# An eleventh weight load split into quarters, two loads held behind the x2 stores, and a top-8 instruction for the choice of experts (one Trainium2 core)

## The reference

```python
def _hmoe(x, g, w_router_group, w_router_expert, w_gate, w_up, w_down):
    xn = _rmsnorm(x, g).reshape(b * l, dm)
    lg = xn @ w_router_group                     # 4 groups
    grp = argmax(lg); wg = max(softmax(lg))
    le_sel = (xn @ w_router_expert)[token, grp]  # 8 experts of the group
    top_v, top_i = lax.top_k(le_sel, 2)
    wk = softmax(top_v) * wg[:, None]
    for e in range(32):
        h = silu(xn @ w_gate[e]) * (xn @ w_up[e])
        y = y + combine[:, e:e + 1] * (h @ w_down[e])
    return x + y
```

## Time and profile before

| what | value |
|---|---|
| median of 3 runs (lowest, highest) | 868.24 us (867.67, 870.07) |
| the profiled execution's own time | 868.5 us |
| span of the profiled execution | 866.9 us |
| TensorE matmul busy | 778.7 us (90%) |
| VectorE, ScalarE, GpSimd busy | 310.0, 136.1, 129.4 us |
| moved by DMA in all | 253.81 MB |
| mean granted TensorE clock | 0.965 |

### The profile page before, as it was taken

One profiled execution on the slowest core, in us unless ns is written; L12 is line 12 of the kernel. 1 busy time (PEld: TensorE's weight loads), 2 busy tenths in 40 slices (PEclk: granted clock), 3 DMA queues, 4 the chain that ended last, 5 costly groups with the idle time before them and its releaser, 6 DMA issues.

```text
span 866.9 us, 9613 instructions
## 1 busy us (share of the span) xinstructions
PE 778.7 (90%) x3736; PEld 430.0 (50%) x3737; DVE 310.0 (36%) x818; ACT 136.1 (16%) x274; POOL 129.4 (15%) x220
## 2 busy tenths in 40 slices
PE   4999999999999999989999878887977977989876
PEld 4888888778877455533333333323323323333222
DVE  4799879624465544631111101101111110111115
ACT  5110021321222333300000000000000000000013
POOL 3000027650233100001111101001000000010100
PEclk9999999999999999999999999889888999989999
DMA  8348033162500790779999999999999999999955
GB/s 283 86 159 139 0 112 100 54 233 92 194 1 1 321 411 27 276 292 422 425 426 425 429 426 426 428 425 427 428 425 428 425 426 429 426 416 407 414 202 246
DMA packets 50784, 253.81 MB, mean 293 GB/s; under 512 B 17829, under 2 KB 18681, under 8 KB 38674
## 3 DMA queue, kind: packets, MB, share of 16 engines
q1 hardware_dynamic: 43778, 239.80, 69.3%
q0 software_dynamic: 6672, 12.86, 4.1%
q10 hardware_dynamic: 288, 0.53, 0.2%
HBM read 246.44 MB, written 14.58 MB: 301 GB/s over the span
## 4 chain that ended last, share of the span: by engine, by line
PE 61%; DMA 31%; SPq 5%; DVE 1%; issue 1%; ACT 1%; POOL 0%; DVEq 0%; ACTq 0%; POOLq 0%
DMA arena<-in_w_exp_up 25%; PE ps L1874 13%; PE ps L1587 13%; PE ps L1650 12%; PE ps L1747 6%; PE ps L1891 6%; SPq L512 3%; PE ps L1963 3%; DMA arena<-x_rows 3%; DMA x_rows<-arena 1%; SPq L516 1%; DMA arena<-in_x_prompt 1%; PE ps L1687 1%; PE ps L1680 1%; PE ps L1864 1%
## 5 line engine op out<-in xcount | busy, mean ns | idle before, releaser
L1874 PE MATMUL ps<-arena 128*64 128x512 f32 x1024 | 249.5, 642 | 55.4 <-DMA arena<-in_w_exp_up 55.3
L1874 PEld LDWEIGHTS ps<-arena 128*64 128x64 f32 x1024 | 81.8, 147 | 200.7 <-issue 192.7
L1891 PE MATMUL ps<-arena 128*64 128x512 f32 x512 | 116.4, 595 | 2.0 <-DVE arena L1485 2.0
L1587 PE MATMUL ps<-arena 128*128 128x272 f32 x480 | 110.8, 393 | 0.0
L1650 PE MATMUL ps<-arena 128*128 128x272 f32 x448 | 105.7, 394 | 1.8 <-ACT arena L758 0.9
L1587 PEld LDWEIGHTS ps<-arena 128*128 128x128 f32 x480 | 91.0, 190 | 18.6
L1489 DVE TENSOR_SCALAR arena<-ps,arena 128x512 f32<-128x512 f32 x32 | 24.0, 751 | 201.1 <-PE ps L1891 201.1
L1650 PEld LDWEIGHTS ps<-arena 128*128 128x128 f32 x448 | 83.9, 190 | 22.3 <-DVE arena L1260 2.6
L1454 DVE TENSOR_TENSOR arena<-ps,arena 128x1024 f32<-128x1024 f32 x15 | 18.4, 1225 | 173.3 <-PE ps L1864 173.3
L907 DVE TENSOR_TENSOR arena<-arena 128x256 f32<-128x256 f32 (+11 forms) x217 | 74.6, 344 | 13.5 <-ACT arena L816 3.9
L857 ACT ACTIVATE arena<-ps,arena 128x512 f32<-128x512 f32 x32 | 22.0, 687 | 306.1 <-PE ps L1874 306.1
(11 more groups left out here) (234 smaller groups left out, 552.7 us busy)
## 6 DMA issues: line engine op xcount, KB each, us to landing
arena<-in_w_exp_gate SPq DMA_DIRECT2D x28, 2048.0 KB, 42.3
arena<-in_w_exp_up SPq DMA_DIRECT2D x28, 2048.0 KB, 32.3
arena<-in_w_exp_down SPq DMA_DIRECT2D x27, 2048.0 KB, 37.9
arena<-in_w_in SPq DMA_DIRECT2D x6, 2048.0 KB, 8.8
arena<-in_w_exp_gate SPq DMA_DIRECT2D x16, 512.0 KB, 11.0
arena<-in_w_exp_up SPq DMA_DIRECT2D x16, 512.0 KB, 18.5
arena<-in_w_exp_down SPq DMA_DIRECT2D x6, 1024.0 KB, 18.4
arena<-in_x_prompt SPq DMA_DIRECT2D x8, 512.0 KB, 9.3
```

Of the source, the lines that this page charges most:

```text
L1587: last = pe.matmul(dst[:, hh, 0:HALF], w[:, k, m * P:(m + 1) * P], rhs[:, k, hh * HALF:(hh + 1) * HALF], start=(k == 0), stop=(k == kk - 1))
L1874: last = pe.matmul(ps[n * TILE:(n + 1) * TILE, 2 + par, :], x_t[:, k, :], w[:, k, :], start=(k == 0), stop=(k == KD - 1))
L1891: last = pe.matmul(ps[half * TILE:(half + 1) * TILE, 6 + par, :], h[par][:, k, :], w_down[:, k, half * F:(half + 1) * F], start=(k == 0), ...
```

## The change

Four edits. (1) Load 10 is cut in four quarters, each of which covers one x2 tile of x_tok. Quarter q is issued when the store of tile q has landed, and the tile has been transposed and squared; three of them stand on SP ahead of load 7, the fourth behind load 9. (2) Loads 8 and 9 also wait until all five x2 stores have landed. (3) POOL waits for the store before, ahead of each x2 store. (4) `choose` takes the two best with `dve.max` (eight largest of a row, sorted) and `dve.max_index` (their positions); `inverse_root` in `norm` becomes a cheaper average of the root and mean/root, whose factor of 2 is put in where rstd is used; one of `keep_busy`'s four rounds goes.

```diff
 def in_quarters(l):
-    return l >= NS and held_before(l) // 3 < QUARTERED and held_before(l) % 3 != 2
+    return l == NS - 1 or l >= NS and held_before(l) // 3 < QUARTERED and held_before(l) % 3 != 2
...
+            def load_over(n):
+                sp.wait_ge(x2_stored, 16 * (n + 1))
+                sp.wait_ge(x2_turned, 2 * n + 2)
+                sp.wait_ge(squares2, 2 * n + 2)
+                q = OUT_ORDER[n]
+                load(NS - 1, slice(q * QUARTER, (q + 1) * QUARTER))
+
+            for n in range(1, TT - 1):
+                load_over(n)
             sp.wait_ge(out_done, 2 * TT - 1)
             load(EARLY)
             sp.wait_ge(out_done, 2 * TT)
+            sp.wait_ge(x2_stored, 16 * TT)
             for l in range(EARLY + 1, NS - 1):
                 load(l)
-            sp.wait_ge(xg_in[0], 16)
-            load(NS - 1)
+            load_over(TT - 1)
...
+                if n:
+                    pool.wait_ge(x2_stored, 16 * n)
                 pool.dma_start(x2_rows[i * P:i * P + ROWS[i]], x_tok[:ROWS[i], i, :]).then_inc(x2_stored, 16)
...
-                inverse_root(mean, root_i)
+                step(dve.reciprocal(tmp, root_i))
+                stt(root_i, mean, tmp, root_i, ALU.mult, ALU.add)
+                step(dve.reciprocal(root_i, root_i))
...
-                def first_max(into, top):
-                    step(dve.tensor_reduce(top[:r], lem_f, X, ALU.max))
-                    stt(hot[:r], lem_f, top[:r], prefer[:r], ALU.is_equal, ALU.mult)
-                    step(dve.tensor_reduce(best[:r], hot[:r], X, ALU.max))
-                    ts(into, hot[:r], best[:r], ALU.is_equal)
-
-                first_max(hot_1, m_1)
-                stt(lem_f, hot_1, -BIG, lem_f, ALU.mult, ALU.add)
-                first_max(hot_2, m_2)
+                step(dve.max(top[:r], lem_f))
+                step(dve.max_index(at_top[:r], top[:r], lem_f))
+                step(dve.tensor_copy(at_two[:r], at_top[:r, 0:2]))
+                for k, hot in enumerate((hot_1, hot_2)):
+                    ts(hot, expert_no[:r], at_two[:r, k:k + 1], ALU.is_equal)
...
             pe.wait_ge(squares2, 2 * TT)
-            keep_busy(4)
+            keep_busy(3)
             ranks(TT - 1)
```

More of the change, by code:

```diff
@@ L274, in encoder_step @@
         slot_val = [small(2, 2 * NE) for _ in range(2)]
-        slot_no, prefer, ebase = small(2, TILE), small(NE), small(NE)
+        slot_no, prefer, ebase = small(2, TILE), small(EG), small(NE)
         row_no = small(TT, 2)
         half_less_1, skip_row = small(1), small(1)
-        lgt, gh, lem, hot = small(36), small(EG), small(EG, EI), small(NE)
-        g_max, g_best, m_1, m_2, best = (small(1) for _ in range(5))
+        lgt, gh, lem = small(36), small(EG), small(EG, EI)
+        top, at_top, at_two, expert_no = small(8), small(8).bitcast(mybir.dt.uint32), small(2), small(NE)
+        g_max, g_best, best = (small(1) for _ in range(3))
         neg_g, neg_1, exps, e_sum, e_2 = small(1), small(1), small(EG), small(1), small(1)
@@ L627, in _ @@
                       allow_small_or_imprecise_dtypes=True)
-            pool.iota(prefer, pattern=[[-1, NE]], base=NE, channel_multiplier=0, allow_small_or_imprecise_dtypes=True)
+            pool.iota(prefer, pattern=[[-1, EG]], base=EG, channel_multiplier=0, allow_small_or_imprecise_dtypes=True)
+            pool.iota(expert_no, pattern=[[1, NE]], base=0, channel_multiplier=0, allow_small_or_imprecise_dtypes=True)
             pool.iota(ebase, pattern=[[EXTRA * TILE, NE]], base=0, channel_multiplier=0,
@@ L838, in exps_out @@
                 act.activation(exps[:r], lgt[:r, 0:EG], ACT.Exp, bias=neg_g[:r], accum_out=e_sum[:r]).then_inc(exp_ready, 1)
-                act.activation(e_2[:r], m_2[:r], ACT.Exp, bias=neg_1[:r]).then_inc(exp_ready, 1)
+                act.activation(e_2[:r], top[:r, 1:2], ACT.Exp, bias=neg_1[:r]).then_inc(exp_ready, 1)
                 act.activation(misc(M_SS + 24, 1), misc(M_ID, 1), ACT.Sqrt if n + 1 < TT else ACT.Silu)
@@ L1344, in norm @@
                 r = ROWS[i]
-                mean, root_i = ss[:r, i:i + 1], rstd[:r, i:i + 1]
+                mean, root_i, tmp = ss[:r, i:i + 1], rstd[:r, i:i + 1], misc(M_SS + 16, 1, r)
                 dve.wait_ge(squares2, 2 * n + 2)
@@ L1360, in choose @@
                 dve.wait_ge(lg_done, n + 1)
-                ts(lgt[:r], ps[:r, 6, 0:36], rstd[:r, i:i + 1], ALU.mult)
+                ts(lgt[:r], ps[:r, 6, 0:36], rstd[:r, i:i + 1], ALU.mult, 2.0, ALU.mult)
                 step(dve.tensor_reduce(g_max[:r], lgt[:r, 0:EG], X, ALU.max))
-                stt(gh[:r], lgt[:r, 0:EG], g_max[:r], prefer[:r, 0:EG], ALU.is_equal, ALU.mult)
+                stt(gh[:r], lgt[:r, 0:EG], g_max[:r], prefer[:r], ALU.is_equal, ALU.mult)
                 step(dve.tensor_reduce(g_best[:r], gh[:r], X, ALU.max))
@@ L1367, in choose @@
                    gh[:r].unsqueeze(2).to_broadcast((r, EG, EI)), ALU.add)
[L1369 to L1377 removed]
+                step(dve.max(top[:r], lem_f))
[3 more added lines that the diff above has]
+                    ts(hot, expert_no[:r], at_two[:r, k:k + 1], ALU.is_equal)
                 dve.tensor_tensor(chosen[n % 2][:r], hot_1, hot_2, ALU.add).then_inc(chosen_ready, 1)
                 dve.tensor_scalar(neg_g[:r], g_max[:r], -1.0, None, ALU.mult)
[L1380 removed]
+                dve.tensor_scalar(neg_1[:r], top[:r, 0:1], -1.0, None, ALU.mult).then_inc(neg_ready, 1)
                 if n >= 2:
@@ L1408, in values @@
                     dve.tensor_scalar(slot_val[n % 2][:r, k, 0:NE], onehot[:r, i, k, :], weight[:r, i, k:k + 1], None, ALU.mult)
-                    last = dve.tensor_scalar(slot_val[n % 2][:r, k, NE:], onehot[:r, i, k, :], rstd[:r, i:i + 1], None, ALU.mult)
+                    last = dve.tensor_scalar(slot_val[n % 2][:r, k, NE:], onehot[:r, i, k, :], rstd[:r, i:i + 1], 2.0, ALU.mult, ALU.mult)
                 last.then_inc(val_ready, 1)
@@ L1479, in _ @@
             step(dve.tensor_copy(ov_entry[:, :, :, 1], weight))
-            dve.tensor_copy(ov_entry[:, :, :, 2], rstd.unsqueeze(2).to_broadcast((P, TT, 2))).then_inc(ov_ready, 1)
+            dve.tensor_scalar(ov_entry[:, :, :, 2], rstd.unsqueeze(2).to_broadcast((P, TT, 2)), 2.0, None, ALU.mult).then_inc(ov_ready, 1)
             def hidden(par, ready):
```

## The result

The changed kernel takes 871.66 us (median of 14 runs, 870.00 to 874.59) against 868.59 us before (14 runs): ratio 1.0031, 95% interval [1.0019, 1.0042]. It is slower: by 2.7 us as the ratio has it, by 3.07 as the two medians stand. (The 868.24 us given ahead is the median of three of these runs of the kernel before.) The forecast was 869.7 us, +0.17%, with a range of 864.4 to 872.2. The profiled execution takes 870.38 us (before 868.5), 1.3 us less than the median of its kernel, and its span is 868.8; so the profiles show the places of the loss, and the runs its size.

What follows compares the result with a forecast made beforehand. The prediction took the weight stream, its unbroken start and remaining bytes, to bound the kernel. First quarters' bytes 1.9 us later, less 0.4, gave +1.5 us on 868.24: 869.7 us, range 864.4 to 872.2.

Steps and rivals of the forecast that it cites:

- no change: Whole kernel: time within about 0.3% (2.6 us) of before; likeliest 869.7 us, own range 868.8 to 870.7; chance 50%.
- slower: First gather held 11.1 us under loads, or low clock lasting longer; 5.8 us later, 873.6 us; chance 20%.
- The stream sets the end: Expert stage: the end depends on when the weight stream runs without pause, at 424 GB/s, and the bytes still to come.
- Holding loads 8 and 9: Before the gather: last x2 store lands in 3.3 us, at 361.9; loads follow, 4.3 us later than before.
- The choice: VectorE's choice of the two best: 1.4 us instead of 2.24, with rows_ready at about 367.95 instead of 368.90.
- The gather lands with the last of the block: First gather, issued at 368.8 among the held loads, lands at 376.0, 1.55 us later than before.
- rival B: First gather gets through between the loads, landing at 372.7; quarters' bytes 3.6 us earlier, 864.6 us; chance 26%.
- Turns of several packets: DMA queues: draining 9 to 17 descriptors per turn would pass the gather's nine or so rows per engine in one turn.
- What TensorE gives back: From the gather's landing to the first quarters of the next loads: 6.0 us at low clock, against 5.56 before.
- If the clock held: TensorE after the gather: with its clock kept up, first quarters would go out 1.8 us sooner than the 5.56.
- The hole is merely moved: Weight stream: load 10 early fills 324.5 to 349.8 us, DMA then idles before the quarters; same bytes and rate afterwards.
- Sum: Whole kernel: quarters' bytes 1.9 us later, less 0.4 already lost before, gives +1.5 us and 869.7 us.

Runs made afterwards that it cites:

- the kernel with the hold and small packets: The changed kernel, still holding loads 8 and 9, with both cut into four quarters (packets of 4 KB instead of 16 KB); ratio 1.0039 to the kernel before.
- the small-packet kernel: The changed kernel with loads 8 and 9 not held and cut into four quarters each (4 KB packets instead of 16 KB); ratio 1.0009 to the kernel before.

## Why the prediction came out as it did

It lay inside the range, with the right sign, at 0.55 of the measured size (+0.17% for +0.31%). The path was the one forecast; its size was short by one term, and one step came out right in part by luck. Its likeliest case was "no change"; the result lies on the bound between that and "slower".

- **The stream sets the end.** Right: 1.10 MB missing at 395 us are 2.6 us, and the stream ends 2.6 us later. The thirteen profiles bear it out where the differences are clear of chance: the four with the fewest MB (29.09 to 29.69) are the four slowest (1.0031 to 1.0047).
- **Holding loads 8 and 9: the last store meets nothing and lands in 3.3 us.** This term was mis-sized. It took 4.6 (4.3 to 4.6 in the five kernels that hold both loads back), and SP issued load 8 another 0.5 us behind the landing, which the forecast had left out: 363.68 instead of 361.9, 1.8 us late. The 3.3 was the shorter of two such stores in the trace before; the one at 322.7 us, without loads as well, took 3.8. With load 8 issued at 363.68 the block runs its 13.5 us and is through at about 377.2, and the gather lands at 377.5 where the forecast had 376.0. Why the store took 4.6 us stays open: 127 of its 144 packets were through by 361.0, 2.5 us behind its issue, and the last ones took until 363.0.
- **The choice.** Right: 1.28 us for 1.4, and rows_ready at 368.06 for 367.95. max and max_index together take 0.48 us from start to end (362.58 to 363.06) for the 0.65 forecast. The Trainium skill ("VectorE: DVE Perf Modes", Two Vector instructions with no wait between them) counts max_index as two instructions, and the trace agrees: MATCH_VALUE_LOAD and FIND_INDEX8. The first takes 0.09 us and runs into the second, and the two take 0.25 from start to end, so 0.25 for each of three, 0.75 in all, would have been 0.27 too much.
- **The gather lands with the last of the block.** Right in outcome: in the changed kernel it lands at 377.5, when the last of the block is through, and at 377.7 and 377.8 in the two other kernels with hold and early quarters. So rival B's landing at 372.7, a gather that gets through between the loads, is out. In part this was luck. The forecast had the gather in turns with the loads from its issue on and left over at their end; in the trace its first packet comes 4 us behind the issue, when about a third of the block is left, and turns of about one packet for one fill the next 4. The late first packet was in no term of the sum. In the kernel with the hold and small packets the gather landed while loads were still moving (0.47 MB of them from 377.5 us on), so its landing isn't tied to the end of the block.
- **Turns of several packets.** The Trainium skill ("DMA: Bandwidth & Descriptors", Queues, rings and completion order) says that a DMA engine drains a whole packet of 9 to 17 descriptors from one queue before it switches. By the reading made of it in rival B the gather's nine or so rows an engine would have gone in one turn. The trace doesn't show it: its 144 packets are spread over 4 us, 373 to 377. The rows aren't listed engine by engine, so turns of fewer than nine aren't shown either.
- **What TensorE gives back.** 5.87 us from landing to first quarters for 6.0. Right. "If the clock held" came true in no run: the clock falls with 0.95 and 1.75 us of idle time too.
- **The hole is merely moved.** Right: the early quarters (315.0 us and on, as forecast) fill the old hole and open one from 375 to 387. Filling it didn't pay in any kernel here.
- **Sum.** 1.5 us was forecast. The gather landed 1.5 us later than forecast and the first quarters went out 1.4 us later (383.36 for 382.0); 1.5 and 1.4 are 2.9, and 2.7 were measured.
- **Slips in the working.** The 1.9 us from issue to bytes comes to 2.0 by its own numbers (382.0 - 374.47 - 5.5), and the lower end of the range names 864.4 as rival B's price, which is 864.6 where it is worked out. Neither changes the forecast.

## What to carry to other kernels

A load that is moved off one small transfer can land on the next, as here: before holding a prefetch, list every small DMA that will be in flight with it, and put the prefetch where none of them is on the path. When a ring is full, loading ahead gained nothing here before the first place came back; keep one load for the time between the last small transfer and that moment. To see where a stream stands, compare the bytes moved up to a fixed time, and divide the difference by the steady rate; know first how far that number moves between kernels that take the same time. And count the packets of two queues only over the time in which both have some: over 361 to 369 us the small-packet kernel shows 661 to 144, over 363 to 365 it shows 109 to 98.

## What the hardware showed that I had not expected

- A store or gather that POOL issued while a block of loads was in flight had its first packet mostly some 4 us later (358.59 to 362.5, 369.01 to 373; 3 and 5 in one kernel), beside 16 KB and 4 KB packets alike; without loads it was 1 to 2 us.
- A store of 0.52 MB beside 16 KB packets of loads took 11.0 to 11.7 us, beside 4 KB packets 8.3 to 8.6, beside one load of 2 MB 8.8, and 2.9 to 5.3 without loads. The gather took 8.5 and 8.3 beside the two kinds of block, 4.0 without loads.
- TensorE's granted clock fell to its lower level with 1.75 us of idle time ahead of the transposes as it did with 4.5 us; four more rounds of `keep_busy` ahead of the idle time changed nothing (1.0031 both times).
- MAX8 took 0.20 us for 128 rows of 32 elements, MATCH_VALUE_LOAD 0.09 and FIND_INDEX8 0.18; a reduction of the same columns took 0.19.
